# A last sum split into two banks, squares and mean in three parts, and the last stores as two copies of 64 rows

## What is computed

```
h = silu(g) * u                      # 256 x 2816, g and u from rmsnorm(x) @ w_in
x = x + 0.5 * (h @ w_out)            # the last sum, 256 x 1024
out = x * rsqrt(mean(x * x) + 1e-6) * norm_final      # mean over the 1024 channels of a token
```

## Time and profile before

| | before |
|---|---|
| median of three runs | 919.99 us |
| the profiled execution's own time | 918.91 us |
| its span, first to last instruction | 917.1 us |
| mean granted clock of TensorE | 0.998 of full |
| TensorE busy | 908.0 us, 99% |
| VectorE, ScalarE, GpSimd busy | 545.8, 482.0, 367.5 us |
| moved by DMA | 165.14 MB, 180 GB/s |

### The profile page before, as it was taken

The page is one execution under the profiler, slowest core; times in us unless marked ns, Lnnn a source line. Parts: engine busy times, 40 slices in busy tenths (PEclk is TensorE's granted clock), DMA queues, the critical chain, the costliest instruction groups (busy, mean ns, idle before and its releaser), DMA issues.

```text
span 917.1 us, 12607 instructions
## 1 busy us (share of the span) xinstructions
PE 908.0 (99%) x4902; PEld 750.1 (82%) x4902; DVE 545.8 (60%) x613; ACT 482.0 (53%) x709; POOL 367.5 (40%) x572
## 2 busy tenths in 40 slices
PE   8999999999999999999999999999999999999997
PEld 7888888888878888888888888888887888888885
DVE  4655665467976556664465555544688755555544
ACT  5644444468666444443564444433578654444433
POOL 4688998862516889988610000000043100000001
PEclk9999999999999999999999999999999999999999
DMA  8975655544257766555455556555534465566541
GB/s 248 261 229 181 189 184 184 181 141 143 96 190 222 211 183 187 186 188 192 149 173 184 184 183 184 184 194 202 165 129 163 128 216 184 185 187 206 183 179 46
DMA packets 130123, 165.14 MB, mean 180 GB/s; under 512 B 18184, under 2 KB 109456, under 8 KB 130064
## 3 DMA queue, kind: packets, MB, share of 16 engines
q1 hardware_dynamic: 129776, 163.81, 56.2%
q10 hardware_dynamic: 288, 0.53, 0.2%
HBM read 163.27 MB, written 1.05 MB: 179 GB/s over the span
## 4 chain that ended last, share of the span: by engine, by line
PE 98%; DMA 0%; issue 0%; POOL 0%; ACT 0%; DVE 0%; POOLq 0%; DVEq 0%
PE bank L387 30%; PE bank L389 30%; PE bank L388 30%; PE bank L452 2%; PE bank L400 1%; PE bank L619 1%; PE bank L649 0%; PE bank L638 0%; PE bank L662 0%; PE bank L726 0%; PE bank L546 0%; DMA cosn<-in_norm_ffn 0%; PE bank L550 0%; PE bank L677 0%; PE bank L755 0%; PE bank L687 0%
## 5 line engine op out<-in xcount | busy, mean ns | idle before, releaser
L1051 DVE TENSOR_TENSOR w_lo<-raw,w_hi 128x1024 fp32r<-128x1024 f32 x303 | 382.0, 1264 | 313.0 <-ACT w_hi L795 312.9
L795 ACT ACTIVATE w_hi<-raw 128x1024 fp32r<-128x1024 f32 x303 | 320.3, 1061 | 305.6 <-PE bank L389 298.6
L387 PE MATMUL bank<-w_hi,x_hi 128*128 128x512 f32 x864 | 341.5, 395 | 0.3 <-DVE x_lo L1066 0.3
L389 PE MATMUL bank<-w_hi,x_lo 128*128 128x512 f32 x864 | 336.9, 390 | 0.0
L388 PE MATMUL bank<-w_lo,x_hi 128*128 128x512 f32 x864 | 336.3, 389 | 0.0
L389 PEld LDWEIGHTS bank<-w_hi,x_lo 128*128 128x128 f32 x864 | 162.1, 188 | 34.5
L387 PEld LDWEIGHTS bank<-w_hi,x_hi 128*128 128x128 f32 x864 | 162.2, 188 | 33.4 <-issue 1.3
L388 PEld LDWEIGHTS bank<-w_lo,x_hi 128*128 128x128 f32 x864 | 162.4, 188 | 32.2
L1289 POOL TENSOR_TENSOR rstd_c<-ms_c,neg_half 128x2 f32<-128x2 f32 (+1 forms) x8 | 5.3, 665 | 399.4 <-DVE ms_c L1071 399.4
L387 PE MATMUL bank<-w_hi,h_hi 128*128 128x512 f32 x352 | 139.0, 395 | 0.0
L389 PE MATMUL bank<-w_hi,h_lo 128*128 128x512 f32 x352 | 137.4, 390 | 0.0
(11 more groups left out here) (158 smaller groups left out, 601.2 us busy)
## 6 DMA issues: line engine op xcount, KB each, us to landing
raw<-in_ffn_w_in SPq DMA_DIRECT2D x172, 512.0 KB
raw<-in_ffn_w_out SPq DMA_DIRECT2D x44, 1024.0 KB
raw<-in_mix_w_in SPq DMA_DIRECT2D x12, 1024.0 KB
raw<-in_mix_w_out SPq DMA_DIRECT2D x8, 1024.0 KB
raw<-in_ffn_w_in SPq DMA_DIRECT2D x8, 256.0 KB, 4.4
gw<-in_ssm_glu_w SPq DMA_DIRECT2D x64, 2.0 KB, 3.5
x<-in_x SPq DMA_DIRECT2D x6, 128.0 KB, 4.4
out<-x SPq DMA_DIRECT2D x6, 128.0 KB, 2.1
```

The source lines that it names most:

```text
L387: mm(o, hi_a, hi_b, start=first, stop=False)
L389: return mm(o, lo_a, hi_b, start=False, stop=last)
L795: A(w_hi[:, n % RING, :], raw[:, s, (n % 2) * 1024:(n % 2) * 1024 + 1024], ACT.Copy).then_inc(hi_done, 1)
L1051: TT(w_lo[:, n % RING, :], raw[:, s, (n % 2) * 1024:(n % 2) * 1024 + 1024], w_hi[:, n % RING, :].bitcast(F32), ALU.subtract).then_inc(lo_d ...
```

## The change

`END_BANK` is the bank pair that the last feed-forward block used for its even up-projection blocks; it is free at the end. Tokens 128 to 255 of channels 768 to 1023 get their last three hidden tiles summed there, in nine matmuls of 256 columns, behind nine matmuls of 256 columns for channels 512 to 767 in the old bank. VectorE adds the whole old bank first (in its upper half that is the sum without the last three tiles) and then the new bank. The squares of block 1 are taken in three parts, its mean in two steps, and its product with the gain in two parts. The four stores of block 1 become two, of 64 partitions each.

```diff
+END_BANK = 2 * ROLES[DEPTH - 1, "ffn2"][0]
...
             sp.wait_ge(fin_done[1], 2)
-            for j in range(2):
-                sp.dma_start(ov[1, j], x[32 * j:32 * j + 32, 1, :]).then_inc(stored, 16)
-            sp.wait_ge(stored, 2 * T * 16)
+            sp.dma_start(ov[1, 0:2], x[0:64, 1, :]).then_inc(stored, 16)
+            sp.wait_ge(stored, (T + 2) * 16)
...
             def end_rows(l, h, pairs):
-                for c, t in ((0, 0), (1, 0), (0, 1), (1, 1)):
-                    tok, w = slice(t * P, t * P + P), slice(c * 512, c * 512 + 512)
+                for c, t, n in ((0, 0, 512), (1, 0, 512), (0, 1, 512), (1, 1, 256)):
+                    tok, w = slice(t * P, t * P + P), slice(c * 512, c * 512 + n)
                     for q in range(END_ROWS):
...
-                        ins = three(bank[2 * pairs[c] + t][:, :], h_hi[:, k, tok], h_lo[:, k, tok],
+                        ins = three(bank[2 * pairs[c] + t][:, 0:n], h_hi[:, k, tok], h_lo[:, k, tok],
                                     w_hi[:, s, w], w_lo[:, s, w], False, q == END_ROWS - 1)
-                        if c and t:
-                            ins.then_inc(half_done, 1)
-                        elif q == END_ROWS - 1:
-                            ins.then_inc(acc_done, 1)
+                    ins.then_inc(acc_done, 1)
+                for q in range(END_ROWS):
+                    s, k = half(l, h + q) % RING, FT - END_ROWS + q
+                    three(bank[END_BANK][:, 0:256], h_hi[:, k, P:2 * P], h_lo[:, k, P:2 * P],
+                          w_hi[:, s, 768:1024], w_lo[:, s, 768:1024], q == 0, q == END_ROWS - 1).then_inc(half_done, 1)
...
+            def end_squares(n, t, c0, c1, to):
+                act.wait_ge(x_done, residuals(DEPTH - 1, ACC_FFN2) + n)
+                if c0:
+                    act.wait_ge(sq_done, 12 * DEPTH + n - 1)
+                A(junk[t][:, 0:c1 - c0], x[:, t, c0:c1], ACT.Square, scale=1.0 / math.sqrt(D),
+                  accum_out=ssq[:, to:to + 1]).then_inc(sq_done, 1)
...
-                act.wait_ge(xg_done, t + 1)
+                act.wait_ge(xg_done, 2 * t + 1)
...
-            for t in range(2):
-                for c in range(2):
-                    end_squares(c, t)
-                end_scale(t)
+            end_squares(1, 0, 0, 512, 0)
+            end_squares(2, 0, 512, 1024, 2)
+            end_scale(0)
+            end_squares(3, 1, 0, 512, 1)
+            end_squares(4, 1, 512, 768, 3)
+            end_squares(5, 1, 768, 1024, 0)
+            end_scale(1)
             ov = out[0].rearrange("(h n j) d -> h j n d", j=T, n=32)
             act.wait_ge(fin_done[1], 2)
-            for j in range(2, T):
-                act.dma_start(ov[1, j], x[32 * j:32 * j + 32, 1, :]).then_inc(stored, 16)
+            act.dma_start(ov[1, 2:4], x[64:128, 1, :]).then_inc(stored, 16)
...
-            def end_gain(t, n):
+            def end_gain(t, n, c0, c1):
                 dve.wait_ge(x_done, residuals(DEPTH - 1, ACC_FFN2) + n)
-                TT(xg[t][:, 512:1024], x[:, t, 512:1024], gfin[:, 512:1024], ALU.mult).then_inc(xg_done, 1)
+                TT(xg[t][:, c0:c1], x[:, t, c0:c1], gfin[:, c0:c1], ALU.mult).then_inc(xg_done, 1)
...
-            end_gain(0, 2)
+            end_gain(0, 2, 512, 1024)
...
+            dve.wait_ge(acc_done, first_sum + 4)
+            end_residual(1, 1)
             dve.wait_ge(half_done, half(DEPTH - 1, DN2 + FT - 1) + 1)
-            end_residual(1, 1)
-            end_gain(1, 4)
+            dve.wait_ge(x_done, residuals(DEPTH - 1, ACC_FFN2) + 4)
+            STT(x[:, 1, 768:1024], bank[END_BANK][:, 0:256], 0.5, x[:, 1, 768:1024], ALU.mult, ALU.add).then_inc(x_done, 1)
+            end_gain(1, 4, 512, 768)
             dve.wait_ge(sq_done, 12 * DEPTH + 4)
-            mean(3 * DEPTH, 1, 2)
+            STT(ms_c[:, 1:2], ssq[:, 1:2], EPS, ssq[:, 3:4], ALU.add, ALU.add).then_inc(ms_part, 1)
+            dve.wait_ge(sq_done, 12 * DEPTH + 5)
+            dve.wait_ge(ms_part, 1)
+            TT(ms_c[:, 1:2], ms_c[:, 1:2], ssq[:, 0:1], ALU.add).then_inc(ms_done, 1)
+            end_gain(1, 5, 768, 1024)
```

More of the change, by code:

```diff
@@ L209, in build @@
         fin_done = [sem("fin_done0"), sem("fin_done1")]
-        xg_done, xg_pool = sem("xg_done"), sem("xg_pool")
+        xg_done, xg_pool, ms_part = sem("xg_done"), sem("xg_pool"), sem("ms_part")
         def by_channel(t, i):
```

## The result

| | before | changed |
|---|---|---|
| median | 919.48 us (4 runs) | 930.7 us (929.07 to 931.01, 4 runs) |
| ratio | | 1.0119, 95% interval 1.0106 to 1.0131 |
| profiled execution, span | 918.91, 917.1 us | 929.07, 927.3 us |
| third addition (512 columns), start, to issue of the last stores | 5.10 us | 4.84 us |
| issue of the last stores to the span's end | 3.60 us | 14.28 us |

The account below looks back on a forecast made before the run. TensorE is 98% of the span, so only the tail could move: +0.12 - 0.21 - 0.21 = -0.30 us to the stores' issue, then stores on two engines, +8.4 us in all on 919.99: 928.4 us, range 922.8 to 932.0.

Parts of the forecast that it names:

- Part 1, matmuls: Last sum on TensorE: nine 512-column matmuls become 18 of 256 columns at 0.12 us each, +0.12 us.
- Part 2, last addition: VectorE's last addition covers 256 columns instead of 512, -0.21 us; the old bank's addition is hidden, 0.1 us in hand.
- Part 3, squares and mean: Last square on ScalarE covers 256 columns, 0.42 us, saving 0.21; partial sum just in time, last product hidden behind GpSimd's power.
- Part 4, engines: Block 1's two stores, outermost count 2, run on 2 DMA engines each instead of 16, both queues sharing the same two.
- Part 4, price: Block 1's stores: 1.05 us to first row, 64 x 0.163 = 10.4 us of data, 0.85 behind; end at 925.5 us.
- rival C: Store rows cost 0.266 us throughout: 17 us of data, +15 us; halfway +11.5, 931.5 us; chance 0.08, half above 932.
- A: All 16 engines still carry each store: store stage shorter by one issue, -0.7 us in all, 919.3 us; chance 0.09.
- B: SP's store and ACT's store use two different engines each, 5.2 us of data: +3.2, 923.2 us; chance 0.08.
- D: 256-column matmuls in the last sum pace at 0.188 us: +1.2 us on any case; with A 920.5 us, chance 0.03.

Follow-up runs that it names:

- experiment 9: Changed kernel with four 32-row stores for block 1, VectorE's last product left out: third addition to issue 4.73 us instead of 4.84, power 0.55 us.
- experiment 3: Changed kernel, two 64-row stores with destination as 64 plain rows, then as 32 by 2 by 1024: ratios 1.0002 and 1.0007, stages 4.19 and 4.22 us.
- experiment 1: Changed kernel with block 1's stores put back to four copies of 32 rows: 918.96 us, ratio 0.9996, stage 3.61 us.
- experiment 5: Changed kernel with SP's 64-row copy kept and ACT's put back to two copies of 32 rows: ratio 1.0063, stage 9.52 us.
- experiment 7: Changed kernel with both 64-row copies issued by SP, then with four 32-row copies of outermost count 2: stages 14.30 and 13.49 us.
- experiment 6: Changed kernel storing only columns 0 to 255 of block 1, in the same two copies with 1 KB rows: stage 5.52 us, span 918.8 us.
- experiment 4: Changed kernel with block 1 stored in one copy of 128 rows on SP, outermost count 4: ratio 1.007, stage 10.51 us.

## Why the prediction was right, point by point

- **Part 1, matmuls.** 0.12 us each and +0.12 in all. Measured: the last matmul starts 1.83 us after the third addition, where it was 1.61, so +0.22; as it is itself shorter (0.28 against 0.39), its end, counted from that addition, came 0.11 later. Right.
- **Part 2, last addition.** -0.21 forecast, -0.27 measured (0.42 for 0.69). The first addition was hidden with 0.2 us to spare.
- **Part 3, squares and mean.** -0.21 forecast and measured (0.42 for 0.63); the partial sum is in time. The last product was costed at nothing, hidden by the power. Its time was hidden, but it made the power 0.11 us longer (experiment 9). With the larger gain of part 2 the sum is -0.26, where -0.30 was forecast.
- **Part 4, engines.** Right in each point: 4 completions, the share of two engines, both queues on the same two (together 51 GB/s, one share of 0.13). The rule read from 248 missing packets of the kernel before held for counts of 2 and 4 and with only the order of the dimensions changed. The Trainium skill states it in "DMA: Bandwidth & Descriptors", section "Why a DMA increments its semaphore by 16 and not by 1", and these traces agree: 4 completions for two copies with a 2 outermost, 4 for one copy with a 4, 32 for two with 32. The share shows that the two queues used the same pair; that it is the lowest-numbered one is shown by no row.
- **Part 4, price.** Here is the term that was mis-sized, "64 rows one after another: 64 x 0.163 = 10.4 us". Measured were 12.3 us (914.3 to 926.6), 0.19 a row. In the first 5.0 us the engines moved 32 GB/s instead of 51, and 5.0 x 19 / 51 is 1.9 us. The wait from issue to first row was 1.27 us, not 1.05, and what follows the last row 0.72, not 0.85. Together +2.0, which is the 14.28 against 12.3. The prediction had seen the sign of it: SP's row price of 0.266 in the earlier trace rows, put down there to slow first rows. In that trace the packets of SP's first 32 rows took 0.34 us each on average and those of its other 32 took 0.19. The sum charged nothing for such a start; the price went into rival C instead, as if it held for all rows. The wait to the first row was put down to the split shape, but the plain copies of 64 rows in experiment 3 waited 1.2 us too.
- **The range.** That 930.7 still lay in it owes something to luck: its upper end, 932.0, came from rival C taken halfway and not from a start of its own size, and 0.8 us of the difference in medians is in neither piece.
- **Rivals.** A (16 engines) was the case to beat, and experiments 1 and 3 show what it would have given: with two wide copies 0.6 us lost on the stores, not 0.4 gained. Its time was wrong in sign, by the pieces of the traces; the medians can't tell it from no change. C, slow rows, was in part true, for 5 us and not throughout. B and D are excluded by the rows above.

Left open is why the first rows of the stage run at some 15 GB/s per engine and the later ones at 25. It isn't one queue alone (experiments 5 and 7), the size of a row (6), the use of just two engines (4) or a second copy beside it (4). Nor is it the whole first copy: with 64 or 128 rows in it the pace rose in its middle, after 5.0 us, and with 32 rows, or 64 short ones, about where it ended, after 3.8 and 2.2 us. The wide stage starts slowly as well, at 202 GB/s in experiment 3 and 291 later. No run told apart whether the delay is in how the first rows are handed to the engines or in the memory that they are written to, and none varied the pause ahead of the stage. It makes up 1.9 of the 10.7 us; the other 8.8 don't hang on it.

## What to carry to other kernels

Before merging copies, look at the outermost count of both sides: a copy here with 2, 4 or 8 outside ran on that many of the 16 engines, so a merge that puts a 2 outside turned 3.6 us of stores into 14.3, while the same addresses with 32 outside took 4.2. The count of completion packets in the profile, 16 for each copy or fewer, shows it for any copy already in the kernel. In a tail of 9 us, cutting the last operand in two returned only 0.26 us, since only the last addition and the last square became shorter (-0.27 and -0.21), and the matmuls and the power gave 0.11 back each.

## What was not expected of the hardware

- For its first 2 to 5 us a stage of narrow stores moved some 15 GB/s per engine, later 25 (29 to 33 against 47 to 53 GB/s on two engines, 55 against 96 on four).
- Of the wide stores neither the fewest nor the most were the fastest: 4.2 us for two of 64 rows, 3.6 for four of 32, 4.1 for eight of 16 (one run).
- GpSimd's power of one column took 0.67 us beside a VectorE product in SBUF and 0.55 without (experiment 9, one run).
